# One more weight buffer in the first MoE, routing tile by tile, and accumulators opened on both sides of the gather

## What is computed

```python
x = x + mixed @ w_out[l]
x = x + hier_moe(rms_norm(x, g_ffn[l]), w_rg[l], ...)

# hier_moe
g_logits = xf @ w_rg + b_rg                       # 4 groups, take the best one
e_logits = xf @ w_re + b_re                       # 8 experts in each group
top_v, top_i = lax.top_k(e_in_group, 2)           # two experts of the best group
for e in range(32):
    hid = jax.nn.silu(xf @ w_gate[e]) * (xf @ w_up[e])
    y = y + combine[:, e:e + 1] * (hid @ w_down[e])
```

## Time and profile before

| | us |
|---|---|
| median of 3 runs | 948.72 |
| lowest and highest of them | 948.4, 950.57 |
| the profiled execution, device time | 948.47 |
| the profiled execution, span of the profile | 946.7 |

### The profile page before, as it was taken

One profiled execution on the slowest core, in us unless ns is written; L12 is line 12 of the kernel. 1 busy time (PEld: TensorE's weight loads), 2 busy tenths in 40 slices (PEclk: granted clock), 3 DMA queues, 4 the chain that ended last, 5 costly groups with the idle time before them and its releaser, 6 DMA issues.

```text
span 946.7 us, 20312 instructions
## 1 busy us (share of the span) xinstructions
PE 798.7 (84%) x9049; PEld 550.7 (58%) x9049; DVE 246.4 (26%) x640; ACT 163.5 (17%) x346; POOL 66.3 (7%) x73
## 2 busy tenths in 40 slices
PE   7999999999999989999998989558576576765765
PEld 4565688884676654446756777446454455544543
DVE  2142930231522221443535121102011020110201
ACT  2012222320411131205624000001000010000100
POOL 6200300000010030350000000000000000000000
PEclk9999999999999999999999999978899797888887
DMA  9985634059699999632657999999999999999996
GB/s 303 325 321 182 239 108 160 1 232 409 234 376 407 407 358 372 235 141 93 256 184 256 409 427 424 426 426 429 429 427 429 429 427 429 430 429 427 429 429 249
DMA packets 55556, 310.15 MB, mean 328 GB/s; under 512 B 5426, under 2 KB 7178, under 8 KB 43088
## 3 DMA queue, kind: packets, MB, share of 16 engines
q1 hardware_dynamic: 50848, 301.60, 79.8%
q0 software_dynamic: 2912, 4.37, 1.6%
q10 hardware_dynamic: 1744, 3.41, 0.9%
HBM read 307.76 MB, written 4.19 MB: 330 GB/s over the span
## 4 chain that ended last, share of the span: by engine, by line
PE 58%; DMA 38%; DVE 2%; issue 1%; ACT 0%; DVEq 0%; SPq 0%; ACTq 0%
PE ps L1630 54%; DMA ring<-in_w_up 27%; DMA ring<-in_w_down 5%; DMA ring<-in_w_gate 5%; PE ps L1656 1%; PE ps L1805 1%; PE ps L1945 0%; PE ps L1670 0%; DMA xx<-in_x 0%; PE ps L2057 0%; PE ps L1687 0%; PE ps L1767 0%; PE ps L1988 0%; DVE xx L1105 0%; PE ps L1678 0%
## 5 line engine op out<-in xcount | busy, mean ns | idle before, releaser
L1630 PE MATMUL ps<-ring,arena 128*32 128x128 f32 (+3 forms) x5792 | 276.6, 335 | 125.4 <-DMA ring<-in_w_up 46.4
L1630 PEld LDWEIGHTS ps<-ring,arena 128*32 128x32 f32 (+1 forms) x5792 | 195.6, 124 | 201.0 <-issue 71.4
L1630 PE MATMUL ps<-ring,xx 128*128 128x512 f32 (+2 forms) x384 | 156.1, 564 | 0.0
L1630 PE MATMUL ps<-arena 32*128 32x256 f32 (+11 forms) x1428 | 133.5, 369 | 5.4 <-issue 2.0
L1630 PEld LDWEIGHTS ps<-ring,xx 128*128 128x128 f32 x384 | 72.1, 190 | 74.9 <-issue 71.1
L1630 PEld LDWEIGHTS ps<-arena 128*32 128x32 f32 (+4 forms) x1428 | 85.8, 164 | 40.2 <-issue 33.4
L874 ACT ACTIVATE arena<-ps 128x128 f32<-128x128 f32 x40 | 11.1, 277 | 426.8 <-PE ps L1630 426.8
L1321 DVE TENSOR_TENSOR arena<-arena,ps 128x128 f32<-128x128 f32 x40 | 11.5, 288 | 277.8 <-ACT arena L874 277.8
L1630 PE MATMUL ps<-xx,ring 128*128 128x256 f32 x288 | 64.9, 382 | 0.0
L1630 PEld LDWEIGHTS ps<-xx,ring 128*128 128x128 f32 x288 | 53.9, 190 | 7.8 <-issue 0.7
L1630 PE MATMUL ps<-ring,xs 128*128 128x512 f32 x96 | 42.8, 604 | 0.0
(11 more groups left out here) (292 smaller groups left out, 575.7 us busy)
## 6 DMA issues: line engine op xcount, KB each, us to landing
ring<-in_w_up SPq DMA_DIRECT2D x38, 2048.0 KB, 25.2
ring<-in_w_gate SPq DMA_DIRECT2D x36, 2048.0 KB, 23.8
ring<-in_w_down SPq DMA_DIRECT2D x33, 2048.0 KB, 24.0
ring<-in_w_in SPq DMA_DIRECT2D x15, 2048.0 KB, 21.5
arena<-in_w_down SPq DMA_DIRECT2D x6, 2048.0 KB, 12.0
ring<-in_w_out SPq DMA_DIRECT2D x4, 2048.0 KB, 8.6
arena<-in_w_gate SPq DMA_DIRECT2D x3, 2048.0 KB, 12.2
arena<-in_w_up SPq DMA_DIRECT2D x2, 2048.0 KB, 15.3
```

The lines of the kernel that those rows point to most:

```text
L1630: ins = pe.matmul(dst, w, x, start=start, stop=stop, skip_group_check=True)
```

## The change

It has three parts.

1. **First MoE, one more buffer.** The up matrix of group 3 is loaded into -4 (`xx`) and no longer into the ring. Its load waits until x is in all four accumulators (`s_open` at 1) and scaled into `xs` (`s_xs` at 4). The ring carries one chunk fewer, so all later chunk numbers are one lower.
2. **Routing tile by tile.** Squares, roots and factors are made for each tile alone (`norm_factors(m, tt)`), and `route_tile(b, tt)` picks experts for one tile. Tile 0's router product moves on PE from behind block 1's last output product into it, and in block 2 ahead of the last product of the dilated branch; the transposes of tile 0 move two products earlier in block 2, into banks 0 and 2. The position products are split into a part for tile 0 and a part for tile 1. One DVE step is saved by counting slots from 1, one moves behind the picks, and one is added ahead of the count of rounds.
3. **Accumulators on both sides.** In block 1 the first of four is opened ahead of tile 1's transposes. In block 2 two are opened ahead of the positions and two behind the gather, and the load into `xx` waits for the last of them (`s_open` at 2) in place of `s_pos`.

```diff
-        AHEAD1 = {2: [S_MOE1 + 3 + n for n in range(3)], 3: [-5, S_MOE1 + 6, S_MOE1 + 7], 4: [-3, -1, -2],
-                  5: [S_MOE1 + 8 + n for n in range(3)]}
+        AHEAD1 = {2: [S_MOE1 + 3 + n for n in range(3)], 3: [-5, -4, S_MOE1 + 6], 4: [-3, -1, -2],
+                  5: [S_MOE1 + 7 + n for n in range(3)]}
...
+                    if g == 3 and n == 1:
+                        sp.wait_ge(s_open, 1)
+                        sp.wait_ge(s_xs, 4)
                     if g == 4 and n == 0:
                         sp.wait_ge(s_gu[0], 2)
...
-            sp.wait_ge(s_pos, 2)
+            sp.wait_ge(s_open, 2)
             sp.wait_ge(s_xs, 6)
             load_moe2(8, 1, SECOND2[8], q1)
...
+                        if k == 1:
+                            act.wait_ge(s_ms, ROOTS[f"x{m}", tt])
+                            act.activation(tile_stat(st_r, tt), tile_stat(st_a, tt), ACT.Sqrt).then_inc(s_rt, 1)
...
+            def route_tile(b, tt):
+                dve.wait_ge(s_rl, 2 * b + tt + 1)
+                step(dve.scalar_tensor_tensor(out=lg[b][:, tt, :], in0=bank(4, NR_COLS, tt * NR_COLS),
+                                              scalar=x_rstd[:, tt:tt + 1], in1=b_route[:, b, :], op0=ALU.mult,
+                                              op1=ALU.add))
+                step(dve.tensor_copy(gl[:, 0:NG], lg[b][:, tt, 0:NG]))
+                step(dve.max(m_tile, gl[:, 0:8]))
+                step(dve.tensor_copy(mg[:, 0:1], m_tile[:, 0:1]))
+                step(dve.match_replace(gr, mg, gl, PICKED))
+                step(dve.tensor_scalar(g_off, gr[:, 0:NG], PICKED, NEG, ALU.not_equal, ALU.mult))
+                step(dve.tensor_tensor(el[:, 0:NE].rearrange("p (g e) -> p g e", g=NG),
...
+                step(dve.max(m_tile, el[:, 0:NE]))
+                step(dve.tensor_copy(me[:, 0:2], m_tile[:, 0:2]))
+                step(dve.match_replace(er, me, el, PICKED))
+                dve.tensor_scalar(sel[b][:, tt, :], er[:, 0:NE], PICKED, None, ALU.is_equal).then_inc(s_sel, 1)
...
-                step(dve.tensor_scalar(posm[:, :, 0:NE], posm[:, :, 0:NE], -1.0, None, ALU.add))
-
+                pick_slots(b, 0)
                 step(dve.tensor_scalar(posm[:, :, NE:], posm[:, :, 0:2 * EG], -float(SLOTS), None, ALU.add))
                 dve.sem_inc(s_posm[b], 1)
-                pick_slots(b, 0)
...
                 step(dve.tensor_reduce(st_a[0:1, 4:5], bank(4, NE)[0:1], AX.X, ALU.max))
+                step(dve.tensor_scalar(st_a[0:1, 4:5], st_a[0:1, 4:5], float(SLOTS), None, ALU.add))
...
                     gather(n)
-                    if not fresh:
+                    if fresh:
+                        open_quarters((2, 3))
+                    else:
                         scatter_expert(val(n * EG), EG - 1)
```

More of the change, by code:

```diff
@@ L1248, in route @@
             def route(b):
-                gl, gr, el, er = route_g[b][:, :, 0, :], route_g[b][:, :, 1, :], route_e[b][:, :, 0, :], route_e[b][:, :, 1, :]
+                el = route_e[b][:, :, 0, :]
                 mg, me = route_m[b][:, :, 0, :], route_m[b][:, :, 1, :]
-                dve.wait_ge(s_rl, b + 1)
-                for tt in range(TT):
-                    step(dve.scalar_tensor_tensor(out=lg[b][:, tt, :], in0=bank(4, NR_COLS, tt * NR_COLS),
-                                                  scalar=x_rstd[:, tt:tt + 1], in1=b_route[:, b, :], op0=ALU.mult,
-                                                  op1=ALU.add))
@@ L1612, in _ @@
             add_product(5, FOX, 1, 0, s_fo)
+            norm_tile(3, R_FFN2, 0)
+            norm_factors(3, 0)
             add_product(6, FOX, 1, 1, s_fo)
@@ L1706, in router, with open_quarters, open_accumulator @@
                              k == 0, k == KD - 1)
-                if tt == 1:
-                    ins.then_inc(s_rl, 1)
+                ins.then_inc(s_rl, 1)
+            def open_quarters(parts):
+                for part in parts:
+                    ins = mm(bank(part), ident, x_sb[:, :, part * T:(part + 1) * T], True, False)
+                if part == 3:
+                    ins.then_inc(s_open, 1)
+            def open_accumulator(b, half, tt):
+                pe.wait_ge(s_xn, 4 * b + 2 * tt + half + 1)
+                ins = mm(bank(2 * tt + half), ident, x_sb[:, tt, half * 512:half * 512 + 512], True, False)
+                if (tt, half) == (1, 1):
+                    ins.then_inc(s_open, 1)
             def normed(m, k):
@@ L1871, in out_product @@
                         norm_tile(1, 0)
-                router(0, 0)
+                open_accumulator(0, 0, 0)
                 norm_tile(1, 1)
             def moe(b, q_base):
-                def open_accumulator(half, tt):
-                    pe.wait_ge(s_xn, 4 * b + 2 * tt + half + 1)
-                    mm(bank(2 * tt + half), ident, x_sb[:, tt, half * 512:half * 512 + 512], True, False)
                 router(b, 1)
                 if b == 0:
-                    open_accumulator(0, 0)
-                    open_accumulator(1, 0)
-                    open_accumulator(0, 1)
-                    open_accumulator(1, 1)
-                else:
-                    for part in range(4):
-                        mm(bank(part), ident, x_sb[:, :, part * T:(part + 1) * T], True, False)
-                pe.wait_ge(s_sel, b + 1)
+                    open_accumulator(0, 1, 0)
+                    open_accumulator(0, 0, 1)
+                    open_accumulator(0, 1, 1)
+                else:
+                    open_quarters((0, 1))
                 before = const[:, C_BEFORE:C_BEFORE + P]
@@ L1894, in moe @@
                 pe.wait_ge(s_nev_d, NEV0[2 * b + 1] + 8)
-                mm(bank(5, 2 * NE), before, sel[b][:, :, :], True, False)
-                mm(bank(5, NE, NE), ones, sel[b][:, 0, :], False, True).then_inc(s_pos, 1)
+                pe.wait_ge(s_sel, 2 * b + 1)
+                mm(bank(5, NE), before, sel[b][:, 0, :], True, True)
+                mm(bank(5, NE, NE), ones, sel[b][:, 0, :], True, False)
+                pe.wait_ge(s_sel, 2 * b + 2)
+                mm(bank(5, NE, NE), before, sel[b][:, 1, :], False, True).then_inc(s_pos, 1)
                 mm(bank(4, NE), ones, sel[b][:, 0, :], True, False)
@@ L2398, in _ @@
             branch_product(DIL, 1, 0, w_dil)
-            pe.wait_ge(s_fo, 4)
-            norm_tile(3, 0)
+            router(1, 0)
             branch_product(DIL, 1, 1, w_dil)
-            router(1, 0)
+            read[0] += 1
             norm_tile(3, 1)
-            read[0] += 1
             moe(1, q1)
```

101 lines of the change are left out of this document (56 added, 45 removed).

## The result

| | before | after |
|---|---|---|
| median of 12 runs each, us | 949.49 (948.4 to 951.35) | 954.37 (952.07 to 958.93) |
| the profiled execution, device time | 948.47 | 953.75 |
| its span | 946.7 | 951.9 |

The ratio of the changed kernel to the one before is 1.0053, 95% interval [1.0044, 1.0063]: 4.9 us slower by the medians, where the forecast's sum said 2.8 us and its range ended at 953.4. The direction was right and the size was not. On the profiles the difference is 5.2 us of span, and the traces say where it lies.

A forecast was written before the change was run, and what follows sets the result against it. DMA was taken to bound the second MoE and PE block 2's mixer. Buffer 0, first routing 0.3 and late load 2.5 summed to 2.8 us on the profiled 948.47; with the median's 0.25, 951.4 us, range 948.4 to 953.4.

The forecast's parts named there:

- The late load: Second MoE: load into xx issued at 515.1 instead of 508.58, 1.06 MB missing by 529, end 2.5 us later.
- a fixed cost for each load: Second MoE: if each queued load paid about 2.0 us fixed, the change would cost 1.9 us more; weighed and rejected.
- At 515.1: Second MoE: forecast issue of the load into xx, 0.35 behind gather and two accumulator openings ending at 514.75.
- PE then gathers (3.75): Second routing: PE's gather takes 3.75 us, then opening two accumulators 1.84, until 514.75.
- Part 1: First MoE, extra buffer: group 3's up moves to about 249, leaving a hole about 263 to 270; gain 0.
- 0.78 + 2.25 = 3.0 us for weights: Late first MoE: PE's two waits for weights, bounding the extra buffer's gain at 3.0 us.
- Part 2, the first routing: Block 1's routing: first MoE starts 0.3 us later, bounds -0.1 to +1.8.
- Part 2, the second routing: Second MoE's routing: last tile's routing starts 1.0 later, sel ready as before, gather 0.8 earlier at 509.15.
- The level of the runs: Whole kernel: median of the runs put 0.25 us above the profiled execution, giving 951.4 to 951.5.
- The load costs its full time: Rival, second routing: price 3.4 + 0.3 us or more, 952.4 to 953.5, slower; chance 0.22.
- The buffer works: Rival, first MoE: group 4's gate goes out earlier, PE's 3.0 us of waits go, 948.5; chance 0.12.
- The routing is really shorter: Rival, both routings: picks 0.8 us earlier twice give 1.6 back, 949.8; chance 0.08.

The follow-up runs named there:

- buffer alone: Kernel before with only group 3's up loaded to xx behind x being in the accumulators; 949.73 us, ratio 0.9997.
- order alone, again: Second sample of the kernel before with group 5's gate loaded ahead of group 4's three chunks, no extra buffer; 948.63 us, ratio 0.9982.
- order alone: Kernel before with group 5's gate loaded ahead of group 4's three chunks, no extra buffer; 947.27 us (10 runs), ratio 0.9962.
- buffer and order: Kernel before with group 3's up to xx and group 5's gate and up loaded ahead of group 4's three chunks; 948.05 us, ratio 0.998.
- changed, early openings: Changed kernel with all four accumulators of the second MoE opened ahead of the positions; 951.89 us, ratio 1.0024.
- changed, early, order: Changed kernel with all four second-MoE accumulators opened ahead of the positions and group 5's gate and up loaded ahead of group 4's; 949.43 us, ratio 0.9985.
- changed again: Changed kernel unaltered, a second sample of time and trace; 954.3 us, ratio 1.0041 to the kernel before.
- changed, filled: Changed kernel with twelve unread 128-column products in PE's four waits between the last branch product and the gather; 952.47 us, ratio 1.003.
- changed and order: Whole changed kernel with gate and up of group 5 loaded ahead of group 4's; 951.78 us, ratio 1.0017.
- late opening alone: Kernel before with two of four second-MoE accumulators opened behind the gather and the load into xx behind them; 955.58 us (6 runs), ratio 1.0056.
- load behind the gather: Kernel before with the load into xx also waiting for the gather's last product, TensorE's instructions unchanged; 953.55 us, ratio 1.0033.
- load one place later: Kernel before with the load into xx also held behind the gather and queued behind down of expert 2; 953.93 us (7 runs), ratio 1.0035.

## Why the prediction was off, point by point

**The issue that decides.** Take the issue of the load into xx, of down of expert 2, and the span:

| kernel | gather, us | load into xx | down of expert 2 | span | span less the issue that decides |
|---|---|---|---|---|---|
| before | 3.84 | 508.58 | 516.62 | 946.7 | 430.1 |
| buffer alone | 3.84 | 508.30 | 516.34 | 946.1 | 429.8 |
| order alone, again | 3.84 | 506.09 | 514.13 | 943.8 | 429.7 |
| order alone | 5.46 | 511.53 | 520.49 | 950.5 | 430.0 |
| buffer and order | 5.46 | 506.84 | 515.80 | 946.1 | 430.3 |
| changed, early openings | 3.84 | 508.72 | 517.29 | 947.9 | 430.6 |
| changed, early, order | 3.84 | 508.28 | 516.85 | 946.9 | 430.1 |
| changed | 5.47 | 517.47 | 519.56 | 951.9 | 434.4 |
| changed again | 5.46 | 517.86 | 519.95 | 952.5 | 434.6 |
| changed, filled | 3.84 | 515.58 | 517.67 | 950.1 | 434.5 |
| changed and order | 5.46 | 516.16 | 518.24 | 950.7 | 434.5 |
| late opening alone | 6.77 | 521.97 | 524.05 | 956.6 | 434.6 |
| load behind the gather | 5.46 | 516.25 | 518.29 | 950.9 | 434.7 |
| load one place later | 5.44 | 519.23 | 518.85 | 952.8 | 434.0 |

Where the load into xx is early (first seven), the end follows the issue of down of expert 2 by 429.7 to 430.6 us. Where it is late and goes out first (the next six), the end follows the load into xx itself by 434.4 to 434.7, over a spread of 6.4 us in that issue. Half of that spread is executions that were late as a whole. Without it, counted from the end of the first MoE as above, the issues lie between 515.1 (filled) and 518.5 (late opening alone), and the spans between 949.6 and 953.1: 3.4 us later, 3.5 us longer. So with this order in the queue every us of lateness is lost one for one, as the forecast held ("from there the DMA engines never rest"). The last row doesn't fit: its order is another, with down of expert 2 first, and the end comes 434.0 behind that, about half a microsecond sooner. In the first 40 us behind the issue it had moved as much as the changed kernel (16.28 MB each); where the half microsecond lies was not found.

**The late load.** With the load at 515.1, as forecast, the end would be at 515.1 + 434.4 = 949.5, which is 2.8 above 946.7, not 2.5. The sum by bytes was 0.3 low, within its bounds, and this part of the mechanism was right. The 1.9 us more that the prediction weighed by a fixed cost for each load did not come. The fit that it took from the Trainium skill (DMA: Bandwidth & Descriptors, Anatomy of one DMA) is stated there for DMAs on GpSimd's path, and these loads are issued by SyncE. Of the 0.3, 0.2 may be the 424 GB/s from 540 to 560 where before had 428 (20 x 4 / 428).

**The issue of that load is the step that failed.** "At 515.1" was 2.4 us early. The trace puts 1.63 of it on the gather (5.47 less 3.84): the term "PE then gathers (3.75)" was too small. It took the duration from a trace in which the clock had stayed at 1.00 up to that point, as did every other row of the sum, and a fall of the clock was put at nothing without a reason. The remaining 0.73 is the state in which the second routing was reached: -0.6 ahead of 198 us, where the two programs do the same work (luck of the execution), -0.3 in the first routing, and +1.6 for the clock behind the wait of 2.27 us at the first MoE's end. Together: 2.84 + 1.63 + 0.73 = 5.2 of span.

**Does the change cause the low clock at the gather?** Not shown. In the fourteen traces of the table the gather ran at 1.2 GHz for part of its time in eight: in four of the five with late openings, the fifth being the filled one, but also in four with TensorE's instructions of the kernel before. Why the clock fell stays open. What the change does cause is the price. With the load issued ahead of the gather, a gather that is 1.62 longer moves down of expert 2 by 0.9 (8.96 behind the load into xx in place of 8.04), since the wait of 0.64 that stood behind the gather takes up the rest; with the load behind the gather it costs the full 1.6.

**And the fall at the first MoE's end?** Of nine traces with the old order of loads and a second wait of 1.6 to 2.5 us, five show a fall behind it, before not among them; of the five with the new order, whose second wait is 0.83 or less, none. That speaks for the wait as its cause, in few traces, and the order's gain is the wait and this fall together; no run separated the two.

**Part 1** was right in its steps: up into xx at 248.12 ("about 249"), a hole from 264 to 269, group 4's gate at 268.78, both waits of PE as before, 0 us. The experiment gave -0.3 per mille with an interval of about 1.2 us to each side. One reading in it was wrong: of the "0.78 + 2.25 = 3.0 us for weights" only the 2.25 is put down to a load, and the 0.78 stayed at 0.79 in both traces of the order alone, so the bound on the gain by weights was 2.25, not 3.0.

**Part 2, the first routing** was forecast 0.3 later and came 0.3 earlier (group 4's gate 0.9 earlier in place of the 0.6 that it brought along). Scaling starts at 243.84 where 244.95 less those 0.6 was expected:

```profile
241.68 1.06 ACT L851 ACTIVATE arena<-xx 128x1024 f32<-128x1024 f32 x1 [8.23 <-DVE xx L1565]
...
242.74 0.61 ACT L855 ACTIVATE xx<-ps,gcol 128x128 f32<-128x128 f32 x2
243.24 0.20 ACT L859 ACTIVATE stat<-stat 128x1 f32<-128x1 f32 x1
243.34 0.61 ACT L855 ACTIVATE xx<-ps,gcol 128x128 f32<-128x128 f32 x2
243.84 3.90 ACT L862 ACTIVATE xs<-xx,stat 128x1024 f32<-128x1024 f32 x2
```

From square to scaling 2.16 us pass, where I had 2.65: the read-out and the copies overlap their neighbours, and the sum of their own rows counted that twice.

**Part 2, the second routing.** The eleven steps for one tile take 2.5 us as forecast (506.44 to 508.94), and from `sel` to the gather 1.3. The gather starts at 510.26, 0.4 later than 509.15 plus the 0.73, and those 0.4 are there at DVE's first step already (506.44 for 505.35 plus 0.73): DVE waits for PE's router product for tile 1, and this now waits for ACT's copies, a wait that the forecast doesn't name.

```profile
504.38 1.95 PE L1661 MATMUL ps<-w_route,xx 128*128 128x36 f32 x16 [0.63 <-ACT xx L855]
```

Behind the gather's start, gather and openings overlap by 0.1 to 0.2, and in the filled kernel the load goes out 5.58 behind the gather's start, where the forecast had 5.95. The two errors cancel, by luck. That the first expert's start is covered in the changed kernel was right as well: down of expert 2 goes out 2.09 behind the load into xx in either clock.

**The level of the runs.** I put the medians at 0.25 above the profiled execution, by three runs. Over 12 runs the median of before was 949.49, over 29 to 32 on other chips 950.3 to 950.4; the profiled execution was near the lowest of all. Of the 3.0 us between 951.4 and 954.37, 0.8 are this (949.49 less 948.72). The other 2.2 can be told from the two profiled executions, which miss the forecast by a like amount (span 951.9 for 949.5): 1.6 twice for the clock and 0.3 for the load, less the 1.2 by which the first half came earlier than forecast (-0.6, and -0.3 in place of +0.3), 2.3 in all. That the medians are made up in the same way is not shown. The profiled execution of before met no fall ahead of the second MoE, and that goes with a low time. The same holds for three more traces (buffer alone 947.9, changed with early openings 949.67, order alone again 945.62), each the fastest run of its kernel and 1.8 to 3.0 us under its median. So the medians hold falls in both kernels, and the forecast started from an execution without any.

**The rivals.** "The load costs its full time" had the right side, but a wrong mechanism: its threshold was an issue later than 515.3, by slow steps on DVE, and these took 2.5 us. It lay nearest to what was measured (952.4 to 953.5) for a reason that it did not have. "The buffer works" named the right place, PE's waits behind the hole in the queue, but the wrong lever: the order alone left group 4's gate where it was and filled the hole ahead of it, and it needed no buffer. "The routing is really shorter" is out for the second routing: with early openings it came 1.1 us later than before.

## What to carry to other kernels

An extra buffer brings its load forward, and a hole stays in the queue unless the next load in order can follow: look at what stands behind it first, since passing one load ahead of a waiting one bought here, by the medians, the 1.7 to 3.0 us that the buffer did not. A load that opens a stage bound by its bytes should not stand behind the last work of the stage before: here each us of that work, at whatever clock, became a us of the total. And a sum made of rows at full clock leaves out the falls that another execution of the same program meets; add what the same instructions cost at the low clock (1.6 us for this gather) on the path that holds the load.

## What the hardware showed that I had not expected

The clock falls in the same program in one execution and not in another: the gather of 32 instructions took 3.84 us in six of the fourteen traces, 5.44 to 5.47 in seven and 6.77 in one, and the stretch behind the first MoE's last long wait 3.88 us in the trace of before and 5.50 in that of the changed kernel. A third such place is the first routing: from 246 to 260 us the clock was 0.88 in four of the fourteen traces and 1.00 in the other ten. Read in quarters of a microsecond from 300 us on, the clock of before, of the changed kernel and of the order alone stands at 1.00 or 0.50 but for single quarters in between; means like 0.60 are mixtures. The Trainium skill (TensorE: Matmul & The Clock Gate, Part 1: The HAM clock gate) describes these two levels and says that the low one is the default, which activity releases; the traces agree in the levels (0.50 and 1.00). That the falls came behind waits agrees with it too (2.27 us, and 0.84 + 0.63 + 0.52 + 0.40 ahead of the gather), but a wait as long in another execution, 2.37 us with the early openings, met none, which no row explains. The median of the same kernel before lay between 949.5 and 950.4 us from one chip and batch to the next, and its runs spread over 5 us, which is as much as this whole change.
